# Two parts of an operand side by side, and wide and narrow matmuls taken in turn

## The reference, cut to what matters

```python
def rmsnorm(x, g):
    xf = x.astype(jnp.float32)
    y = xf * lax.rsqrt(jnp.mean(xf * xf, axis=-1, keepdims=True) + EPS)
    return (y * g.astype(jnp.float32)).astype(x.dtype)

def swiglu(h, w_in, w_out):
    gate, up = jnp.split(h @ w_in, 2, axis=-1)
    return (jax.nn.silu(gate) * up) @ w_out

def chunked_sgu(h, w_in, v_norm, w_s, b_s, w_out):
    bsz, seq, _ = h.shape
    z = jax.nn.gelu(h @ w_in)
    u, v = jnp.split(z, 2, axis=-1)
    ...
    return (u * gate) @ w_out
```

## Time, and the profile before

| | |
|---|---|
| time, median of 3 runs | 2850.55 us (2849.43 to 2851.61) |
| time of the profiled execution | 2843.43 us |
| its span, from first to last instruction | 2841.6 us |
| mean granted clock of TensorE | 0.962 of 2.4 GHz |
| TensorE busy | 2642.1 us, 93% of the span |
| TensorE weight loads busy (beside the matmuls) | 1943.3 us, 68% |
| VectorE busy | 1443.3 us, 51% |
| ScalarE busy | 959.4 us, 34% |
| DMA | 698.81 MB, 246 GB/s on average |

### The profile page before, as it was taken

How to read it: one execution, slowest core, us unless ns; L and a number is a source line. 1 busy time by engine, 2 the same in 40 slices (tenths; PEclk the granted TensorE clock), 3 DMA queues, 4 the chain that set the end, 5 groups by cost and what they waited for, 6 DMA issues and landing times. The chain is left out here.

```text
span 2841.6 us, 41126 instructions
## 1 busy us (share of the span) xinstructions
PE 2642.1 (93%) x16296; PEld 1943.3 (68%) x16297; DVE 1443.3 (51%) x1981; ACT 959.4 (34%) x1146; POOL 7.5 (0%) x12
## 2 busy tenths in 40 slices
PE   7999799999989989689999999999999789988998
PEld 6898788988978977554444444444444378777988
DVE  6846568487468647533244222221222457355893
ACT  4425345365326422411111221121222272123662
POOL 0000000000000000000000000000000000000000
PEclk9999899999999999869999999999999899989999
DMA  7664646657375531179979999999989533342452
GB/s 229 231 231 130 231 140 213 229 164 252 119 252 173 213 149 60 21 316 414 420 310 419 419 420 419 420 420 421 420 353 388 217 104 119 124 172 89 148 192 74
DMA packets 259080, 698.81 MB, mean 246 GB/s; under 512 B 18449, under 2 KB 177885, under 8 KB 209661
## 3 DMA queue, kind: packets, MB, share of 16 engines
q1 hardware_dynamic: 258498, 695.89, 64.7%
q10 hardware_dynamic: 474, 1.37, 0.2%
HBM read 696.16 MB, written 1.05 MB: 245 GB/s over the span
## 5 line engine op out<-in xcount | busy, mean ns | idle before, releaser
L836 DVE TENSOR_TENSOR weight_parts<-weight_slots,weight_parts 128x2048 fp32r<-128x2048 f32 x208 | 473.7, 2288 | 176.1 <-ACT weight_parts L830 173.8
L2807 PE MATMUL bank<-weight_slots,item_x 128*64 128x512 f32 x2176 | 497.3, 605 | 22.3 <-DMA weight_slots<-in_w_mlp 22.3
L830 ACT ACTIVATE weight_parts<-weight_slots 128x2048 fp32r<-128x2048 f32 x208 | 393.4, 1909 | 244.0 <-DMA weight_slots<-in_ffn_w_out 77.2
L1041 PE MATMUL bank<-h_parts,weight_parts 128*128 128x512 f32 x1536 | 389.3, 395 | 0.0
L2807 PEld LDWEIGHTS bank<-weight_slots,item_x 128*64 128x64 f32 x2176 | 152.1, 138 | 314.5 <-issue 288.1
L2982 DVE TENSOR_TENSOR expert_sum_then_keys<-bank,expert_sum_then_keys 128x512 f32<-128x512 f32 x136 | 84.5, 684 | 496.3 <-PE bank L2851 496.3
L848 PE MATMUL bank<-hidden_high,weight_parts 128*128 (+1 forms) x1760 | 308.3, 279 | 8.9 <-DVE weight_parts L836 8.9
L1041 PEld LDWEIGHTS bank<-h_parts,weight_parts 128*128 128x128 f32 x1536 | 274.7, 188 | 51.3
L848 PEld LDWEIGHTS bank<-hidden_high,weight_parts 128*128 128x128 f32 x1760 | 270.0, 190 | 9.9 <-issue 9.9
L2838 PE MATMUL bank<-weight_slots,item_act 128*64 128x512 f32 x1088 | 246.5, 607 | 6.6 <-DVE item_act L2975 3.2
L848 PE MATMUL bank<-hidden_low,weight_parts 128*128 (+1 forms) x880 | 245.6, 279 | 0.0
(11 more groups left out here) (574 smaller groups left out, 3168.9 us busy)
## 6 DMA issues: line engine op xcount, KB each, us to landing
weight_slots<-in_w_mlp SPq DMA_DIRECT2D x384, 1024.0 KB, 17.3
weight_slots<-in_ffn_w_in SPq DMA_DIRECT2D x88, 1024.0 KB, 5.2
weight_slots<-in_ffn_w_out SPq DMA_DIRECT2D x44, 1024.0 KB, 7.2
weight_slots<-in_ffn_w_up SPq DMA_DIRECT2D x22, 1024.0 KB, 5.2
weight_slots<-in_a_w_in SPq DMA_DIRECT2D x16, 1024.0 KB, 6.8
weight_slots<-in_w_in SPq DMA_DIRECT2D x16, 1024.0 KB, 5.6
weight_slots<-in_ffn_w_down SPq DMA_DIRECT2D x11, 1024.0 KB, 7.2
weight_slots<-in_a_w_out SPq DMA_DIRECT2D x8, 1024.0 KB, 16.2
```

The source lines that it names most:

```text
L830: K.nc.scalar.activation(high, source, ACT.Copy).then_inc(K.high_written.sem, 1)
L836: K.nc.vector.tensor_tensor(low, place, high.bitcast(F32), ALU.subtract)\
L1041: K.nc.tensor.matmul(ps, high[k], pair[:, :, k, :], start=k == 0, stop=False, skip_group_check=True)
L2807: m = nc.tensor.matmul(ps[c // 2][half(c % 2), :], x[:, s, :], ring.slot(s)[:, c * 512:(c + 1) * 512], start=s == 0, stop=s == 7, skip_gro ...
```

## The change

The tensor `h_parts` changes its layout from [part, tile k, token] to [tile k, part, token]. The 256 high and the 256 low columns of one feature tile, which were two runs of 1 KB with 8 KB from one start to the next, become one run of 2 KB. The two instructions that write the parts get a destination of eight runs of 256 elements in place of one run of 2048. And `columns_by_parts` issues wide, narrow, wide, narrow, tile by tile.

```diff
@@ dense_up, and the same in feed_forward
-    with nc.sbuf_tensor("h_parts", [P, 2, DT, S], F32R, allow_name_mangling=True) as pair, \
+    with nc.sbuf_tensor("h_parts", [P, DT, 2, S], F32R, allow_name_mangling=True) as pair, \
...
-        h_high, h_low = pair[:, 0, :, :], pair[:, 1, :, :]
+        h_high, h_low = pair[:, :, 0, :], pair[:, :, 1, :]
...
-                    write_high(K, flat(h_high), flat(src[:, :, :]))
+                    write_high(K, h_high, src[:, :, :])
...
-                    leave_low(K, dve, K.high_written(2), flat(src[:, :, :]), flat(h_high), flat(h_low))
+                    leave_low(K, dve, K.high_written(2), src[:, :, :], h_high, h_low)
@@ columns_by_parts
-    high, low = ([w[:, k * 256 + half * P:k * 256 + (half + 1) * P] for k in range(DT)] for w in weights)
     for k in range(DT):
-        K.nc.tensor.matmul(ps, high[k], pair[:, :, k, :], start=k == 0, stop=False, skip_group_check=True)
-    for k in range(DT):
-        last = K.nc.tensor.matmul(ps[:, 0:S], low[k], pair[:, 0, k, :], start=False, stop=k == DT - 1, skip_group_check=True)
+        high, low = (w[:, k * 256 + half * P:k * 256 + (half + 1) * P] for w in weights)
+        K.nc.tensor.matmul(ps, high, flat(pair[:, k, :, :]), start=k == 0, stop=False, skip_group_check=True)
+        last = K.nc.tensor.matmul(ps[:, 0:S], low, pair[:, k, 0, :], start=False, stop=k == DT - 1, skip_group_check=True)
     return last
```

More of the change, by code:

```diff
@@ L1185, in feed_forward @@
         hid_low = parts_view(nc, f"hidden_low{K.vsteps.n}", shape)
-        pair = stack.enter_context(nc.sbuf_tensor("h_parts", [P, 2, DT, S], F32R, allow_name_mangling=True))
-        h_high, h_low = pair[:, 0, :, :], pair[:, 1, :, :]
+        pair = stack.enter_context(nc.sbuf_tensor("h_parts", [P, DT, 2, S], F32R, allow_name_mangling=True))
+        h_high, h_low = pair[:, :, 0, :], pair[:, :, 1, :]
         if part is not None:
@@ L1290, in _ @@
             norm.await_operand(act)
-            write_high(K, flat(h_high), flat(K.h[:, :, :]))
+            write_high(K, h_high, K.h[:, :, :])
             norm.root(act)
@@ L1332, in _ @@
             split(0, 0, 1, first_up[0][1], 3)
-            leave_low(K, dve, K.high_written(2), flat(K.h[:, :, :]), flat(h_high), flat(h_low))
+            leave_low(K, dve, K.high_written(2), K.h[:, :, :], h_high, h_low)
             norm.invert(dve)
```

## The result

The changed kernel takes 2858.65 us (median of 7 runs, 2852.26 to 2861.12), the one before 2848.5 us in the 7 runs beside them (2845.29 to 2851.61). The ratio is 1.0038, with an interval from 1.0026 to 1.005: slower by 0.4%, some 10 us, where 16 us less than before were forecast.

The account below looks back on a forecast made before the run. TensorE's matmul stream was taken as the bound. A pair falling from 346.3 to 336 ns saves 1536 x 10.3 = 15.8 us, other terms 0: 2850.55 - 15.8 = 2834.7, say 2835 us; range 2821 to 2850.

Parts of the forecast that it names:

- VectorE kept its lead: Expert-free stretches: VectorE runs 4.4 us ahead, goes from 78% to 81% busy and does not become the bound.
- the split of h: VectorE's writing of h_parts in eight runs: 1.7 us of cover in the first swiglu, cost taken as 0.
- the 336 forecast: Pair of one 512-column and one 256-column matmul: 220 + 116 = 336 ns, 10.3 less than before.
- the narrow one: 256-column matmul behind a 512-column one: between 113.8 and 118 ns, the middle, 116, taken.
- the second is the layout: Up products: each run of moving columns costs 6 to 7 ns, so a 512-column matmul with one run takes 220 ns.
- The row that I had set aside: Line 2118, plain fp32, eight runs of 64: 1024 cycles plus 3 ns, so a run costs nothing there; discounted for fp32r.
- Memory Cachelines: Skill section: SBUF reads run at full rate with two accesses per 16-byte line, so the new layout brings nothing.
- the first is the order: Up products, old layout, wide and narrow alternating: 225 + 118 = 343 to 344 ns a pair, 3 to 5 us saved.
- A worse phase, slower: Rival, chance 0.1: alternating pairs fall into the bad spacing step, 354 ns a pair, +11.8 us, 2862 us.

Follow-up runs that it names:

- the stream kernel: Kernel without the computation, streams of 24 matmuls or pairs on an idle chip: 226.7 ns for 512 columns, 119.6 for 256, 353.3 for an alternating pair.
- the address runs: Operand starts shifted: the grid; changed kernel, h_parts 96 bytes on, 0.9997; kernel before, h_parts 128 bytes on, 0.999, and two more tensors shifted, 0.9986; ratios to kernel before.
- the grid: Kernel without the computation: narrow, wide, alternating and run-of-seven streams at 8 by 8 operand starts, 32 bytes apart; an alternating pair took 346.7 to 354 ns.

## Why the prediction was wrong

It was right on what surrounds the stream. TensorE's spacing passes to the end one to one: 1536 x 6.3 = 9.7 us by the spacings, 10.2 us in the medians. No wait appeared, VectorE kept its lead, the split of h cost nothing, and a narrow one behind a wide one stayed at 118. The pair came out 17.2 ns above the 336 forecast: 9.8 in what a wide one costs by the order (234.8 in place of 225), 5 in the layout and 2.4 in the narrow one, for which I took 116.

**The step that failed in size is "the second is the layout".** I took it that every run of moving columns costs 6 to 7 ns and put a wide one with one run at 220. Layout alone changed nothing (346.9 a pair in both), and in the stream kernel one run and two runs both took 226.7. It was the largest term, 5 of the 10.3 ns forecast (225 to 220; the order had 3.3 and the narrow one 2). The row that I had set aside, plain fp32 with eight runs of 64, pointed the right way, and so did the section "Memory Cachelines" of the Trainium skill's "Advanced Engine Details and Errata", quoted in the prediction. My reason against them, that a format of two cycles a column hides a break, was a guess without a row. That the excess stays at 13.3 ns for 256, 320, 384 and 512 columns shows that it is an amount for each matmul.

**The step that failed in sign is "the first is the order".** It took the wide one that stands between eight narrow ones and the next wide one (225 then, 226.2 by all starts) as the price of every wide one behind a narrow one. In turn it costs 234.8. The row was read rightly and carried to a place where it doesn't hold: that matmul has a narrow one ahead of it but a wide one behind it. The opposite boundary stood in the same trace. The last wide one of eight, with a narrow one behind it, takes 235.5, which the short windows of the earlier trace rows show as 0.24 and which the prediction spread over its mean of 233.6. Counted together, the boundaries between runs bring nothing: 7.1 ns less for the wide one behind narrow ones, 2.2 more for the wide one ahead of a narrow one, 4.8 more for the narrow one behind it. In turn every wide one is of both kinds at once, and the trace of before could not say which value wins; it was the second. Order alone showed the full cost, 353.2 a pair.

What happened is the rival "A worse phase, slower", at 354 ns and 2862 us, to which I gave a chance of 0.1; it came out at 353.2 and 2858.65. That spacing depends on place is what the address runs show, but the row that it was taken from doesn't: the 113 and 117 ns of the down stages change from trace to trace with nothing moved. That it named the outcome is in part luck. The price of 225 that spoke against it was the same misplaced row.

The cause as the runs show it: an fp32r matmul here has an excess over its columns, often a whole number of steps of 6.67 ns on average. Its size depends on the difference of the start addresses of moving and stationary operand modulo 256 bytes, on the loads between the matmuls (with 64 columns in the wide one's load the cost of alternation goes), and on what ran before. In the kernel, at a difference of 192, alternation costs about one step more a pair than runs of eight; in turn at 32 the pair is back at 346.9. The bf16 and plain fp32 streams had an excess of only 2.4 to 2.6 ns and no cost of alternation; their starts were not varied.

What stays open: what in the hardware makes the steps; why the same operands have two steady patterns and what chooses between them; why a load under 384 columns cost more than one under 256; why the grid's cell doesn't give the kernel's 346.9 in runs of eight.

## What to carry to other kernels

When two formats or lengths of matmul share a stream, take the cost of a pattern from a trace of that pattern; one boundary between two runs doesn't give the price of alternating. Look at both boundaries between two runs, since a gain at one can be paid at the other. In an fp32r stream a few ns a matmul that didn't scale with its columns had nothing to do with how contiguous they were; before rewriting the order of such a stream, shift one operand by 32 to 224 bytes and look at the spacing of the starts, since this alone moved an alternating pair between 346.7 and 354 ns. Look at more than one stage and one trace, since the same stream can run at 113 or at 117 ns. And where the stream is close to what another engine can feed, as in the layer with the convolution, a faster stream becomes a wait.

## What the runs showed of the hardware that was not expected

- fp32r: 512 columns take 226.7 to 235 ns and 256 columns 113.3 to 120, by the addresses, the neighbours and what ran before; bf16 takes 215.8 and 109.1, plain fp32 429.1 and 215.9.
- Two separate runs of 1 KB and one of 2 KB read equally fast (226.7 and 226.7), and a destination of eight runs costs VectorE nothing (2.28 against 2.29 us).
- The spacing of an fp32r stream depends on the difference of the operands' starts modulo 256 bytes (in most cells of the grid, whichever of the two is moved); shifts of 256 or 512 bytes change it by less than 1 ns.
- The same alternating stream on the same operands ran at 353.3 in one kernel and at 346.7 in another, and the same down stage at 113.3 to 113.8 in some traces and at 117.4 to 117.8 in others.
